# List matmuls moved between turning and multiplying the second listed expert; expert weights reloaded in two steps

## The chip, the cores and the metric

One core of one Trainium2 chip runs the whole program. The metric is the device time of one execution in microseconds (us), the median of three runs. Five engines work side by side, each in its own program order: PE (TensorE), DVE (VectorE), ACT (ScalarE), POOL (GpSimd) and SP (SyncE), which here issues DMAs. They order each other by semaphores that count up (`wait_ge`, `then_inc`). Sixteen DMA engines carry all transfers.

## The reference, cut to what matters

Two layers, 1024 tokens of width 1024, float32. Each layer is a mixer (layer 0: latent attention and a convolution; layer 1: sparse attention) and then a mixture of experts. The change lies in the mixture alone, which both layers run:

```
group   = top 1 of 4 groups by h @ router_group
experts = top 2 of the 8 experts of that group by h @ router_expert
y(token) = sum over its 2 experts e of gate * ((silu(h @ w_gate[e]) * (h @ w_up[e])) @ w_down[e])
x = x + y
```

There are 32 experts with a hidden width of 256. `w_gate[e]`, `w_up[e]` and `w_down[e]` are 1 MB each, so that every layer reads 96 MB of expert weights.

## The kernel before, in words

**Routing.** `route_and_experts` (L1329) first ranks each token inside its expert and sorts the experts by their load. PE's part: 48 matmuls of no use (`spin`, L1323), three matmuls that count tokens (L1657 to L1661), then 16 matmuls of one column for each of the first two experts (L1666) which give the row lists of these two "fast" units early, and 40 more spins. DVE makes one-hot masks (`row_hot`, L1922; `token_hot`; POOL makes `gate_hot`, L1527), and PE multiplies them into the complete lists of rows and gates (32 matmuls at L1679, the "list matmuls"). DVE copies their result to `index` and `gates` (`lists`, L1928 and L1929), and POOL can then gather the rows of all other units.

**Units.** The experts are worked off in 25 units, n = 0 to 24: 18 wide ones (one expert, up to 128 rows) and 7 pairs (two experts, 64 rows each), in the order 4 wide, then seven times (pair, wide, wide). Pairs are units 4, 7, 10, 13, 16, 19 and 22. For a unit PE does:

- `turn_first(n)` (L1572): 8 transposes of the gathered rows, which ACT and DVE copy to `x_cols` (`copy_x`, L1708 and L1715);
- `gate_up(n)` (L1591 wide, L1603 pair): gate and up products. It waits for the whole of the unit's weights (`w_here`, all three transfers) and for the copies;
- `down(n)` (L1633, L1644): the product with `w_down`. ACT and DVE weigh it to `y` (`weigh_y`, L1724 and L1794), and POOL adds `y` to the tokens in DRAM by an indirect DMA (L1489), one such DMA at a time.

In the steady loop the order on PE is gate_up(n+1), turn_first(n+2), down(n). Ahead of it, units 0 and 1 are written out by hand: turn 0, gate_up 0, turn 1, gate_up 1, list matmuls, down 0, turn 2, down 1, gate_up 2, turn 3.

**Weights.** Six buffers of 3 MB hold one expert each. Load i (0 to 31) goes to buffer i % 6; wide units take one load, pairs two. Loads 0 to 5 are issued early. SP then issues load i for i = 6 to 31 as soon as `down_done` tells that the unit that used load i-6 has ended its down product (L1458, L1459): gate, up and down in one go (`load_expert`, L1298). `LOADS[i][0]` is the unit of load i. Load 6 waits for unit 0, load 7 for unit 1, load 8 for unit 2, loads 10 and 11 for unit 4.

**Rows.** Four buffers hold gathered rows. POOL issues the gather of unit n+6 at unit n (`gather_first`, L1474), after the transposes that free the buffer; those of units 2 to 5 directly behind `lists`.

Of the kernel before, what the change touches and what calls it, by code (L numbers as in the profile page):

```python
# [1224 lines left out]
WEIGHT_BUFS = 6  # L1225
# [71 lines left out]

def load_expert(eng, A, layer, e, w, here):  # L1298

    gate, up, down = (A[n][layer] for n in ("moe_w_gate", "moe_w_up", "moe_w_down"))  # L1300
    eng.dma_start(w[:, GATE, :], gate[bass.ds(e, 1)].rearrange("o (p c) f -> p (o c f)", p=P)).then_inc(here, 16)
    eng.dma_start(w[:, UP, :], up[bass.ds(e, 1)].rearrange("o (p c) f -> p (o c f)", p=P)).then_inc(here, 16)
    eng.dma_start(w[:, DOWN, :].rearrange("p (c n) -> p c n", c=2), down[bass.ds(e, 1)].rearrange("o (c p) n -> p (o c) n", p=P)).then_inc(here, 16)


def load_place(eng, A, layer, i, order, w, w_here):

    n, place = LOADS[i]
    e = eng.value_load(order[place:place + 1, 0:1], min_val=0, max_val=EXPERTS - 1)
    load_expert(eng, A, layer, e, w[i % WEIGHT_BUFS], w_here[i % WEIGHT_BUFS])  # L1310

# [10 lines left out]
def spin(pe, ident, spare, count):  # L1322

    for _ in range(count):
        pe.transpose(spare[:, 0:P], ident[:, :], ident[:, :])  # L1325


def route_and_experts(nc, name, layer, logits, w, w_here, ident, ones, index, order, order_ready, more, gates, extra_end, turn_no,
# [8 lines left out]
    with Phase(nc, name) as ph:  # L1337
# [115 lines left out]
        with nc.Block() as block:  # L1453
            @block.sync
            def _(sp):
                loads(sp)
                for i in range(B, EXPERTS):
                    sp.wait_ge(down_done, LOADS[i - B][0] + (LEAD + 1))  # L1458
                    load_place(sp, A, layer, i, order, w, w_here)  # L1459
                if load_next:  # L1460
                    sp.wait_ge(down_done, LAST_SHARED_UNIT + (LEAD + 1))
                    load_next(sp)

                def extra(j):
                    sp.wait_ge(down_done, j + (UNITS + LEAD))
                    e = sp.value_load(more[0:1, bass.ds(j, 1)], min_val=0, max_val=EXPERTS - 1)
                    load_expert(sp, A, layer, e, w[0], w_here[0])

                extras(sp, extra)
# [94 lines left out]
            def _(pe):  # L1564
# [83 lines left out]
                def down(n):  # L1648
                    if paired(n):
                        down_pair(n)  # L1650
                    else:
                        down_wide(n, buffers(n)[0], n % 2)

                spin(pe, ident, spare, 48)
                pe.wait_ge(exps_ready, 3)
# [5 lines left out]
                pe.matmul(rank_ps[:, 0:T * EXPERTS], ones[:, :], so_far[:, :, :].rearrange("p e t -> p (e t)"),  # L1661
                          start=False, stop=True).then_inc(ranked, 1)
                for n in range(FAST):
                    pe.wait_ge(fast_hot_ready, n + 1)
                    for t in range(T):
                        last = pe.matmul(fast_ps[n][:, 0:1], fast_hot[:, n, t, :], token[:, t:t + 1], start=(t == 0), stop=(t == T - 1))  # L1666
                    last.then_inc(fast_listed, 1)
# [3 lines left out]
                turn_first(1)  # L1671
                gate_up(1)
                for k in range(TOP_K):
# [8 lines left out]

                down(0)
                turn_first(2)
                down(1)
                gate_up(2)
                turn_first(3)
                for n in range(FAST, UNITS):
                    if n + 1 < UNITS:
                        gate_up(n + 1)  # L1690
                    if n + 2 < UNITS:
                        turn_first(n + 2)
                    down(n)
                    if n + 1 < UNITS and paired(n + 1):
                        turn_hidden(n + 1)
# [15 lines left out]
            def _(act):  # L1711
# [18 lines left out]
                for n in range(FAST):  # L1730
                    copy_x(act, copy, n, n, 0, x_act)
                    copy_x(act, copy, n, n, 1, x_dve)
                    sigmoid(n, n)
                act.wait_ge(lists, 1)
                weigh_y(0, 0, gates[:, 0:1])
                copy_x(act, copy, 2, 0, 0, x_act)
                weigh_y(1, 1, gates[:, 1:2])
                sigmoid(2, 0)
                copy_x(act, copy, 3, 1, 0, x_act)
                for n in range(FAST, UNITS):  # L1740
                    u = SEQUENCE[n]
                    if n + 1 < UNITS:
                        sigmoid(n + 1, (n + 1) % 2)
                    if n + 2 < UNITS:
                        copy_x(act, copy, n + 2, n % 2, 0, x_act)
                    if n >= 2:
                        act.wait_ge(y_sent, 16 * (n - 1))
# [13 lines left out]
            def _(dve):  # L1761
# [153 lines left out]
                for k in range(TOP_K):  # L1915
# [4 lines left out]
                    for half in range(2):  # L1920
# [3 lines left out]
                                          ).then_inc(row_hot_ready, 1)  # L1924
                for n in range(FAST):
                    hidden(n)
                dve.wait_ge(indexed, 1)
                mine.link(dve.tensor_scalar(index[:, :], index_ps[:, 0:BLOCKS], no_token[:, 0:1], None, ALU.add))  # L1928
                dve.tensor_copy(gates[:, :], index_ps[:, BLOCKS:2 * BLOCKS]).then_inc(lists, 1)  # L1929
                dve.wait_ge(lists, 1)  # L1930
                weigh_y(0, 0, gates[:, 0:1])
                copy_x(dve, dve.tensor_copy, 2, 0, 1, x_dve)
                weigh_y(1, 1, gates[:, 1:2])
                count_extra()
                hidden(2)
                copy_x(dve, dve.tensor_copy, 3, 1, 1, x_dve)
                for n in range(FAST, UNITS):
                    u = SEQUENCE[n]
# [1139 lines left out]
```

## Time and profile before

| | us |
|---|---|
| median of 3 runs | 2223.14 |
| lowest, highest | 2219.01, 2225.81 |
| the profiled execution's own time | 2218.28 |
| its span in the profile | 2216.4 |
| PE busy | 1977.6 (89%) |
| DVE, ACT, POOL busy | 951.6, 701.8, 458.6 |

The profiled execution is one run under the hardware profiler; the time of 1.9 us outside its span is start and end. "Granted clock" is the share of full speed that TensorE was given: 1.00 is 2.4 GHz and 0.50 is 1.2 GHz. "DMA share" is the mean busy share of the 16 DMA engines (it can come out a little above 1). The routing and expert stage of layer 0 stands at about 614 to 979 us, that of layer 1 at about 1853 us to the end. PE's idle time in front of a group stands in square brackets with what ended it; "issue" there means that nothing the profile shows was waited for, and at a pair's first gate_up matmul (L1603) it is the wait for weights to land, which this view does not name.

### The profile page before, as it was taken

What the parts mean: (1) busy time and instruction counts of PE and PEld (TensorE: products, weight loads), DVE (VectorE), ACT (ScalarE), POOL (GpSimd) and SP (SyncE); (2) the same over time, 40 slices, a digit from 0 to 9 for tenths busy, and PEclk for the clock granted to TensorE, in tenths of its full rate; (3) what the DMA queues carried; (4) which work ended last, traced back from release to release, by engine and by line L of the source; (5) the groups of instructions that cost most, each with busy time, mean ns of one, the idle gap of its engine ahead of it and who ended that gap; (6) DMA issues with size and microseconds to landing.
All of it is one profiled execution on the core that took longest, in us unless ns stands there. A gap on an engine that the chain in (4) does not pass through costs nothing. (4 is left out here: it accounts for less than half of the span.)

```text
span 2216.4 us, 30271 instructions
## 1 busy us (share of the span) xinstructions
PE 1977.6 (89%) x11237; PEld 1260.0 (57%) x11237; DVE 951.6 (43%) x2308; ACT 701.8 (32%) x1765; POOL 458.6 (21%) x619
## 2 busy tenths in 40 slices
PE   6999859999989988959999858999999998998987
PEld 3444435655587656545655535666666457675664
DVE  3896874433252211104223486666665126211111
ACT  4013655531111111112122575766776111111111
POOL 0001003321022212110000254554454001221211
PEclk9999969999989999989999888999999998999999
DMA  5000011132568999863000200001000515799993
GB/s 219 0 0 0 0 32 36 39 119 85 233 231 326 377 364 369 314 218 56 1 0 0 80 1 11 11 11 49 11 21 11 205 64 233 270 361 379 362 335 120
DMA packets 80888, 307.77 MB, mean 139 GB/s; under 512 B 18352, under 2 KB 23495, under 8 KB 63846
## 3 DMA queue, kind: packets, MB, share of 16 engines
q1 hardware_dynamic: 66342, 272.23, 31.7%
q0 software_dynamic: 14400, 33.59, 6.1%
q8 instruction: 92, 1.51, 0.3%
q14 instruction: 54, 0.44, 0.1%
HBM read 276.75 MB, written 47.89 MB: 146 GB/s over the span
## 5 line engine op out<-in xcount | busy, mean ns | idle before, releaser
L1112 POOL TENSOR_SCALAR nsaatt_probs<-nsaatt_probs,nsaatt_inv,trunk_gates_or_logits 128x384 f32<-128x384 f32 (+7 forms) x256 | 186.5, 742 | 201.4 <-DVE nsaatt_inv L1139 201.4
L1125 DVE CUSTOM_DVE_ANT_0 nsaatt_probs<-nsaatt_scores,trunk_arena 128x384 f32<-128x384 f32 (+7 forms) x256 | 151.3, 629 | 87.7 <-PE nsaatt_scores L1031 87.4
L1766 DVE TENSOR_TENSOR experts_sig<-experts_gu_ps,experts_sig 128x256 f32<-128x256 f32 x50 | 21.2, 425 | 372.1 <-ACT experts_sig L1720 372.1
L1083 ACT ACTIVATE nsaatt_probs<-nsaatt_probs,nsaatt_bias 128x384 f32<-128x384 f32 (+7 forms) x256 | 169.4, 669 | 11.8 <-DVE nsaatt_bias L1134 11.7
L1591 PE MATMUL experts_gu_ps<-experts_x_cols,ahead 128*128 128x128 f32 x1408 | 161.8, 276 | 5.5 <-ACT experts_x_cols L1715 5.5
L1591 PEld LDWEIGHTS experts_gu_ps<-experts_x_cols,ahead 128*128 128x128 f32 x1408 | 159.1, 192 | 12.1 <-issue 12.0
L1031 PE MATMUL nsaatt_scores<-layer_k_cols,trunk_x_rows 64*128 64x384 f32 (+3 forms) x640 | 131.1, 521 | 15.7 <-DVE nsaatt_top L1125 12.8
L1041 PE MATMUL nsaatt_turn<-trunk_ident,nsaatt_probs 128*128 128x128 f32 x912 | 123.8, 279 | 23.7 <-POOL nsaatt_probs L1112 6.0
L1720 ACT ACTIVATE experts_sig<-experts_gu_ps 128x256 f32<-128x256 f32 x50 | 19.2, 384 | 379.4 <-PE experts_gu_ps L1591 242.1
L1041 PEld LDWEIGHTS nsaatt_turn<-trunk_ident,nsaatt_probs 128*128 128x128 f32 x912 | 97.2, 140 | 57.5 <-issue 36.7
L2250 PE MATMUL nsain_q_ps<-trunk_arena,l1b_h_cols 128*128 128x512 f32 x256 | 111.7, 594 | 0.0
L268 DVE SCALAR_TENSOR_TENSOR l0a_conv<-layer_v_rows,l0a_taps,l0a_conv 128x1024 f32<-128x1024 f32 x87 | 104.8, 1284 | 0.0
L1474 POOL DMA_INDIRECT moe_x<-h_rows,moe_index x46 | 47.7, 1036 | 271.6 <-PE experts_x_ps L1572 240.7
L563 DVE TENSOR_TENSOR trunk_x_rows<-out_acc,trunk_x_rows 128x512 f32<-128x512 f32 x32 | 22.1, 692 | 171.7 <-PE out_acc L491 171.7
L1087 ACT ACTIVATE trunk_arena<-nsaatt_turn 128x512 f32<-128x512 f32 (+1 forms) x136 | 65.8, 515 | 79.6 <-PE nsaatt_turn L1041 78.9
L1031 PEld LDWEIGHTS nsaatt_scores<-layer_k_cols,trunk_x_rows 64*128 64x128 f32 x640 | 55.1, 195 | 60.3 <-issue 37.3
L1724 ACT ACTIVATE trunk_x_rows<-experts_y_ps,moe_gates 128x512 f32<-128x512 f32 x50 | 34.4, 688 | 157.2 <-PE experts_y_ps L1633 99.7
L1054 PE MATMUL nsaatt_values<-trunk_arena,layer_v_rows 128*64 128x128 f32 x1228 | 81.8, 276 | 0.0
L2250 PEld LDWEIGHTS nsain_q_ps<-trunk_arena,l1b_h_cols 128*128 128x128 f32 x256 | 48.2, 190 | 58.0 <-issue 57.9
L1633 PE MATMUL experts_y_ps<-ahead,experts_hid 128*128 128x512 f32 x176 | 79.4, 594 | 2.0 <-DVE trunk_x_rows L1794 2.0
L1031 PE MATMUL mlaatt_scores<-layer_k_cols,trunk_x_rows 96*128 96x512 f32 (+3 forms) x192 | 74.9, 530 | 5.1 <-DVE mlaatt_top L1125 4.1
L1603 PE MATMUL experts_gu_ps<-ahead,experts_x_cols 128*64 128x512 f32 x192 | 61.8, 654 | 19.4 <-issue 19.4
(444 smaller groups left out, 3774.6 us busy)
## 6 DMA issues: line engine op xcount, KB each, us to landing
ahead<-in_moe_w_gate_dram SPq DMA_DIRECT2D x34, 1024.0 KB, 12.0
ahead<-in_moe_w_up_dram SPq DMA_DIRECT2D x34, 1024.0 KB, 16.4
ahead<-in_moe_w_down_dram SPq DMA_DIRECT2D x34, 1024.0 KB, 22.7
trunk_arena<-in_moe_w_gate_dram SPq DMA_DIRECT2D x10, 1024.0 KB, 7.5
trunk_arena<-in_moe_w_up_dram SPq DMA_DIRECT2D x10, 1024.0 KB, 14.1
trunk_arena<-in_moe_w_down_dram SPq DMA_DIRECT2D x10, 1024.0 KB, 23.2
moe_w<-in_moe_w_gate_dram SPq DMA_DIRECT2D x10, 1024.0 KB, 9.6
moe_w<-in_moe_w_up_dram SPq DMA_DIRECT2D x10, 1024.0 KB, 14.5
```

Of the source, the lines that this page charges most:

```text
L268: ins = dve.scalar_tensor_tensor(out=to, in0=shifted, scalar=w, in1=to, op0=ALU.mult, op1=ALU.add)
L1031: last = pe.matmul(scores_of(s, r, h)[:, lo:hi], st["q"][h], br["k"][h](lo, hi), start=True, stop=True)
L1041: last = pe.transpose(t_ps[n % TURNS][:, (h * (hi - lo) + b - lo) * P:(h * (hi - lo) + b - lo + 1) * P], part(s, r, h)[:, b * P:(b + 1) * ...
L1054: last = pe.matmul(o_ps[h * V_DIM:(h + 1) * V_DIM, 0:P], br["v"][h](b), turned_probs[n % PT_BUFS][:, at:at + P], start=(r == 0 and b == 0) ...
L1083: act.activation(part(s, r, h), part(s, r, h), ACT.Exp, bias=bias[:, b, i:i + 1], scale=steps[s]["scale"][h], accum_out=total[:, b, i:i + ...
L1087: return act.activation(to, source, ACT.Copy)
L1112: pool.tensor_scalar(part(s, r, h), part(s, r, h), inv[:, s % BUFS, i:i + 1], 1.0 if gate is None else gate[h], ALU.mult, ALU.mult).then_i ...
L1125: dve.tensor_tensor_reduce(part(s, r, h), scores_of(s, r, h), br["mask"], 1.0, -3e38, ALU.add, ALU.max, top[:, s % BUFS, i:i + 1]).then_in ...
L1591: last = pe.matmul(to, wm[:, c, half * P:(half + 1) * P], x_cols[:, b, c, :], start=(c == 0), stop=(c == CHUNKS - 1))
L1603: last = pe.matmul(gu_ps[b][mine, :].rearrange("p (k f) -> p k f", k=2), x_cols[:, b, c, mine], w[s][:, GATE:UP + 1, c * HIDDEN:(c + 1) * ...
L1633: last = pe.matmul(y_ps[half][:, :], hid[:, b, c * P:(c + 1) * P], wm[:, c, half * BANK:(half + 1) * BANK], start=(c == 0), stop=(c == 1))
L2250: last = pe.matmul(to, h_cols[:, c, t * P:(t + 1) * P], w_in[:, c, lo:hi], start=(c == 0), stop=(c == CHUNKS - 1))
```

## The change

PE's order for units 0 and 1: the list matmuls now stand behind turn 1 and ahead of gate_up 1, and from there the steady loop runs from n = 0 (gate_up 1, turn 2, down 0, gate_up 2, turn 3, down 1, ...). ACT, DVE follow: ACT's sigmoid of unit 1 and DVE's `hidden(1)` move behind `lists`, and DVE makes `count_extra` ahead of it. The first spin goes from 48 to 60 matmuls, and 16 spins are added between the counting matmuls and the one-column matmuls. The reload of a buffer is split: gate and up wait for `gu_done` of the unit that used the buffer, and down, issued behind them on the same queue, for its `down_done`. The whole diff:

```diff
--- before.py
+++ after.py
@@ -1295,19 +1295,21 @@
         eng.wait_ge(self.x_stored, 16 * TILES)
 
 
-def load_expert(eng, A, layer, e, w, here):
+def load_expert(eng, A, layer, e, w, here, down_free=None):
 
     gate, up, down = (A[n][layer] for n in ("moe_w_gate", "moe_w_up", "moe_w_down"))
     eng.dma_start(w[:, GATE, :], gate[bass.ds(e, 1)].rearrange("o (p c) f -> p (o c f)", p=P)).then_inc(here, 16)
     eng.dma_start(w[:, UP, :], up[bass.ds(e, 1)].rearrange("o (p c) f -> p (o c f)", p=P)).then_inc(here, 16)
+    if down_free:
+        eng.wait_ge(*down_free)
     eng.dma_start(w[:, DOWN, :].rearrange("p (c n) -> p c n", c=2), down[bass.ds(e, 1)].rearrange("o (c p) n -> p (o c) n", p=P)).then_inc(here, 16)
 
 
-def load_place(eng, A, layer, i, order, w, w_here):
+def load_place(eng, A, layer, i, order, w, w_here, down_free=None):
 
     n, place = LOADS[i]
     e = eng.value_load(order[place:place + 1, 0:1], min_val=0, max_val=EXPERTS - 1)
-    load_expert(eng, A, layer, e, w[i % WEIGHT_BUFS], w_here[i % WEIGHT_BUFS])
+    load_expert(eng, A, layer, e, w[i % WEIGHT_BUFS], w_here[i % WEIGHT_BUFS], down_free)
 
 
 def load_router(nc, layer, w, bias, here, A):
@@ -1455,8 +1457,9 @@
             def _(sp):
                 loads(sp)
                 for i in range(B, EXPERTS):
-                    sp.wait_ge(down_done, LOADS[i - B][0] + (LEAD + 1))
-                    load_place(sp, A, layer, i, order, w, w_here)
+                    last_use = LOADS[i - B][0] + (LEAD + 1)
+                    sp.wait_ge(gu_done, last_use)
+                    load_place(sp, A, layer, i, order, w, w_here, (down_done, last_use))
                 if load_next:
                     sp.wait_ge(down_done, LAST_SHARED_UNIT + (LEAD + 1))
                     load_next(sp)
@@ -1651,7 +1654,7 @@
                     else:
                         down_wide(n, buffers(n)[0], n % 2)
 
-                spin(pe, ident, spare, 48)
+                spin(pe, ident, spare, 60)
                 pe.wait_ge(exps_ready, 3)
                 pe.wait_ge(carry_made, 2)
                 pe.matmul(rank_ps[:, 0:T * EXPERTS], not_before[:, :], member[:, :, :].rearrange("p e t -> p (e t)"),
@@ -1660,6 +1663,7 @@
                 pe.matmul(total_ps[:, 0:EXPERTS], ones[:, :], so_far[:, :, T - 1], start=True, stop=True).then_inc(ranked, 1)
                 pe.matmul(rank_ps[:, 0:T * EXPERTS], ones[:, :], so_far[:, :, :].rearrange("p e t -> p (e t)"),
                           start=False, stop=True).then_inc(ranked, 1)
+                spin(pe, ident, spare, 16)
                 for n in range(FAST):
                     pe.wait_ge(fast_hot_ready, n + 1)
                     for t in range(T):
@@ -1669,7 +1673,6 @@
                 turn_first(0)
                 gate_up(0)
                 turn_first(1)
-                gate_up(1)
                 for k in range(TOP_K):
                     pe.wait_ge(token_hot_ready, k + 1)
                     pe.wait_ge(gate_hot_ready, k + 1)
@@ -1680,12 +1683,7 @@
                                          start=(k == 0 and t == 0), stop=(k == TOP_K - 1 and t == T - 1))
                 last.then_inc(indexed, 1)
 
-                down(0)
-                turn_first(2)
-                down(1)
-                gate_up(2)
-                turn_first(3)
-                for n in range(FAST, UNITS):
+                for n in range(UNITS):
                     if n + 1 < UNITS:
                         gate_up(n + 1)
                     if n + 2 < UNITS:
@@ -1730,19 +1728,16 @@
                 for n in range(FAST):
                     copy_x(act, copy, n, n, 0, x_act)
                     copy_x(act, copy, n, n, 1, x_dve)
-                    sigmoid(n, n)
-                act.wait_ge(lists, 1)
-                weigh_y(0, 0, gates[:, 0:1])
-                copy_x(act, copy, 2, 0, 0, x_act)
-                weigh_y(1, 1, gates[:, 1:2])
-                sigmoid(2, 0)
-                copy_x(act, copy, 3, 1, 0, x_act)
-                for n in range(FAST, UNITS):
+                    if n == 0:
+                        sigmoid(0, 0)
+                for n in range(UNITS):
                     u = SEQUENCE[n]
                     if n + 1 < UNITS:
                         sigmoid(n + 1, (n + 1) % 2)
                     if n + 2 < UNITS:
                         copy_x(act, copy, n + 2, n % 2, 0, x_act)
+                    if n == 0:
+                        act.wait_ge(lists, 1)
                     if n >= 2:
                         act.wait_ge(y_sent, 16 * (n - 1))
                     weigh_y(n, n % 2, gates[:, u:u + 1])
@@ -1922,19 +1917,13 @@
                         dve.tensor_tensor(row_hot[:, k, part], over(row_no[:, :].unsqueeze(1), (P, HALF_TILES, P)),
                                           over(row_f[:, k, part].unsqueeze(2), (P, HALF_TILES, P)), ALU.is_equal
                                           ).then_inc(row_hot_ready, 1)
-                for n in range(FAST):
-                    hidden(n)
+                hidden(0)
                 dve.wait_ge(indexed, 1)
                 mine.link(dve.tensor_scalar(index[:, :], index_ps[:, 0:BLOCKS], no_token[:, 0:1], None, ALU.add))
                 dve.tensor_copy(gates[:, :], index_ps[:, BLOCKS:2 * BLOCKS]).then_inc(lists, 1)
                 dve.wait_ge(lists, 1)
-                weigh_y(0, 0, gates[:, 0:1])
-                copy_x(dve, dve.tensor_copy, 2, 0, 1, x_dve)
-                weigh_y(1, 1, gates[:, 1:2])
                 count_extra()
-                hidden(2)
-                copy_x(dve, dve.tensor_copy, 3, 1, 1, x_dve)
-                for n in range(FAST, UNITS):
+                for n in range(UNITS):
                     u = SEQUENCE[n]
                     if n + 1 < UNITS:
                         hidden(n + 1)
```

## Rows read from the trace of the kernel before

**Rows 1.** The page: busy time of each engine:

```profile
PE 1977.6 (89%) x11237; PEld 1260.0 (57%) x11237; DVE 951.6 (43%) x2308; ACT 701.8 (32%) x1765; POOL 458.6 (21%) x619
```

**Rows 2.** Waits, PE in both expert stages (us in total, times, longest):

```profile
PE experts_gu_ps L1603 <- issue: 20.2, 5, 9.2
...
PE experts_gu_ps L1603 <- issue: 18.8, 5, 7.0
```

**Rows 3.** Timeline of PE, layer 0: start, length, line, [idle before]:

```profile
614.24 6.95 PE L1325 MATMUL experts_gu_ps<-trunk_ident 128*128 128x128 f32 x48 [1.10 <-PEq L448]
621.02 0.64 PE L1657 MATMUL experts_y_ps<-experts_member,experts_not_before 128*128 128x256 f32 x2
...
624.19 3.57 PE L1666 MATMUL experts_hid_ps<-experts_token,trunk_x_rows 128*128 128x1 f32 x16 [1.58 <-DVE trunk_x_rows L1858]
627.63 3.55 PE L1666 MATMUL experts_index_ps<-experts_token,trunk_x_rows 128*128 128x1 f32 x16
631.04 6.20 PE L1325 MATMUL experts_gu_ps<-trunk_ident 128*128 128x128 f32 x40
637.08 1.04 PE L1572 MATMUL experts_x_ps<-trunk_ident,moe_x 128*128 128x128 f32 x8
...
649.15 7.38 PE L1591 MATMUL experts_gu_ps<-experts_x_cols,ahead 128*128 128x128 f32 x64 [1.38 <-ACT experts_x_cols L1715]
656.37 3.70 PE L1679 MATMUL experts_index_ps<-trunk_arena,trunk_x_rows 128*128 128x86 f32 x32
659.90 3.63 PE L1633 MATMUL experts_y_ps<-ahead,experts_hid 128*128 128x512 f32 x8
665.70 1.16 PE L1572 MATMUL experts_x_ps<-trunk_ident,moe_x 128*128 128x128 f32 x8 [2.17 <-DMA moe_x<-h_rows,moe_index]
...
679.64 7.38 PE L1591 MATMUL experts_gu_ps<-experts_x_cols,trunk_arena 128*128 128x128 f32 x64 [1.31 <-DVE experts_x_cols L1708]
```

**Rows 4.** Timeline of PE, the same stretch of layer 1:

```profile
1864.76 1.95 PE L1666 MATMUL experts_hid_ps<-experts_token,trunk_x_rows 128*128 128x1 f32 x16 [1.52 <-DVE trunk_x_rows L1858]
...
1876.05 1.04 PE L1572 MATMUL experts_x_ps<-trunk_ident,moe_x 128*128 128x128 f32 x8
...
1904.84 1.16 PE L1572 MATMUL experts_x_ps<-trunk_ident,moe_x 128*128 128x128 f32 x8 [2.34 <-DMA moe_x<-h_rows,moe_index]
```

**Rows 5.** Windows, long stretches and clock, layer 0; last row layer 1:

```profile
628.00:630.00 2.00, 2.00 (x11) 0.50 0.00 0
648.00:720.00 72.00, 67.38 (x458) 1.00 0.76 276
720.00:808.00 88.00, 77.73 (x475) 0.96 1.02 377
...
1864.00:1866.00 2.00, 1.24 (x11) 1.00 1.05 438
```

**Rows 6.** Timeline of DVE and SP in layer 0: last row mask, first reloads:

```profile
645.54 1.85 DVE L1922 TENSOR_TENSOR trunk_x_rows<-experts_row_no,experts_row_f 128x512 f32<-128x512 f32 x2
...
664.28 0.34 SPq L1301 DMA_DIRECT2D ahead<-in_moe_w_gate_dram  x1
...
692.09 0.34 SPq L1301 DMA_DIRECT2D ahead<-in_moe_w_gate_dram  x1
```

**Rows 7.** Windows: length, PE busy, granted clock, DMA share, GB/s; layer 0:

```profile
640.00:648.00 8.00, 7.77 (x70) 1.00 1.02 414
656.00:664.00 8.00, 7.54 (x45) 1.00 0.09 17
680.00:696.00 16.00, 16.00 (x101) 1.00 0.77 280
```

**Rows 8.** DMA issues of 640 to 960 us: count, median us to landing:

```profile
moe_x<-h_rows,moe_index POOLq DMA_INDIRECT x23, 8.5
```

**Rows 9.** Timeline of PE, layer 0: pairs of units 10 and 13:

```profile
762.44 7.09 PE L1603 MATMUL experts_gu_ps<-ahead,experts_x_cols 128*64 128x512 f32 x32 [1.05 <-issue]
...
806.86 1.09 PE L1603 MATMUL experts_gu_ps<-moe_w,experts_x_cols 128*64 128x512 f32 x1 [9.22 <-issue]
```

## The prediction, made before the changed kernel ran

> **What bounds the kernel now.** I read the page first: PE is busy 89% of the span [rows 1], so what counts is where PE still waits. The list of waits over the two expert stages gives one large group: pairs whose first gate_up matmul stands for 20.2 us in layer 0 and 18.8 us in layer 1, five times each [rows 2]. These are waits for weights. The timeline of PE then shows three short holes at the head of the units [rows 3]: 1.38 us ahead of gate_up 1 (copies of the turned rows; gate_up 0, which is not touched, waits alike), 2.17 us ahead of turn 2 (the gather that could only start behind the lists), 1.31 us ahead of gate_up 3 (copies again). Layer 1 has the same holes, with 2.34 us at turn 2 [rows 4]. Last the DMA windows: from 720 to 808 us the DMA engines are full (share 1.02) while PE is not, and before that, 648 to 720, they stand at 0.76 [rows 5]. So the stage has two regimes: a head set by PE's order, and behind it a stretch set by how early the weight transfers were started.
>
> **Part 1, list matmuls ahead of gate_up 1.** Turn 1 ends at 649.15 - 1.38 = 647.77 [rows 3]. The last row mask is ready at 645.54 + 1.85 = 647.39 [rows 6], so the list matmuls can start at once. They take 659.90 - 656.37 = 3.53 us, and the 1.38 us of copies of unit 1 lie under them: that hole goes. Copies of unit 3 lie under down 1 in the new order, as in the loop: the 1.31 us goes. Turn 2 now comes behind gate_up 1 (656.37 - 649.15 = 7.22 us). Before, it started 665.70 - 659.90 = 5.80 us after the end of the lists, with the DMA engines idle (share 0.09 from 656 to 664 [rows 7]); 5.80 is under 7.22, so with this landing time 2.17 us goes too. Removed: 4.86 us in layer 0, 1.38 + 2.34 + 1.31 = 5.03 us in layer 1.
>
> The cover is thin, 1.4 us. The gathers over the whole stage take a median of 8.5 us [rows 8], and the first reload now runs beside these four. The gather of unit 2 took 4.3 us at the idle engines; with 8.5 it would come 4.2 us later, and PE would stand 4.2 - 1.4 = 2.8 us. I take 1.5 us of new wait per layer (only gate and up of one load are in flight), between 0 and 2.8. `hidden(1)` and `count_extra` ahead of it on DVE lie under gate_up 1 and cost nothing; the weighing of unit 0 follows them and is needed only by down 1, one gate_up later.
>
> The Trainium skill bears on this place, page "DMA: Bandwidth & Descriptors", section "Issuing engines are not separate DMA queues": transfers started by SP and by GpSimd run on the same 16 engines and interleave. It speaks against the change, and the trace agrees: 4.3 us idle, 8.5 us in the median. By that rule the 2.8 us would be due in both layers, and at its worst it is the slower rival below.
>
> **Part 2, spins.** The counting matmuls start when the 48 spins end: 621.02 - 614.24 = 6.78 us, 0.141 each. Twelve more cost 1.7 us, on the path, since DVE's masks wait for the counts. The 16 spins (2.3 us) fill the 1.58 us hole ahead of the one-column matmuls [rows 3] and overrun it by some 0.5 us. The one-column matmuls then start up to 1.7 + 0.5 = 2.2 us later; so I take it for layer 1, and 1.8 for layer 0, where some 0.4 us of counting was a wait for DVE. Against that stands the clock: in layer 0 it was 0.50, 1.2 GHz [rows 5], and the 32 took 631.04 - 624.19 = 6.85 us; in layer 1 it was 1.00 at first [rows 5] and the first 16 took 1.95 us [rows 4], so 32 of them take 3.9 us at 2.4 GHz. The 40 spins behind them took 6.04 us, 5.7 at full clock. All warm: layer 0 gains 2.95 + 0.35 - 1.8 = 1.5 us; layer 1, where the one-column matmuls and spins took 1876.05 - 1864.76 = 11.3 us and would take 3.9 + 5.7 = 9.6, loses 2.2 - 1.7 = 0.5. All cold as before: they lose 1.8 and 2.2. I take layer 0 -1.1 and layer 1 +0.8 (the clock still falls somewhere in the run), together -0.3; both ends kept: -1.0 to +4.0. The gather of unit 0 is no obstacle: like unit 2's it needs some 4.3 us and PE spins past it.
>
> **Part 3, reload in two steps.** Gate and up of load 6 leave when gate_up 0 is done, about 647, not at 664.28 [rows 6]. Its down waits for down 0, at nearly the old time. From then on SP is one unit ahead: gate and up of load 7 leave right behind down 6, those of load 8 when down 1 ends, about 674, against 692.09 [rows 6]. The new wait in front of each down holds back the next load's gate and up, but these would have waited for the same unit or a later one before. No transfer leaves later except by PE's order (down 1 now ends some 3 us later: load 7's last third).
>
> What is it worth? Loads arrive at the pace of full engines from 720 on, so an arrival moves forward by the DMA work that is now done in what was idle: in 648 to 720 that idle is (1.02 - 0.76) x 72 / 1.02 = 18.4 us [rows 5]. Filled are: 2.1 MB of gate and up at 414 GB/s [rows 7] = 5.1 us; some 1 us from load 7; the idle of 680 to 696, (1.02 - 0.77) x 16 / 1.02 = 3.9 us [rows 7], by load 8. Sum 10.0 us. The pair of unit 13, which waited 9.22 us after 1.05 us at unit 10 [rows 9], had 10.3 us of waits, and PE reaches it 3 to 5 us sooner by part 1, so the DMA decides there and unit 13 starts 10 us sooner. Behind it the remaining waits, 20.2 - 10.3 = 9.9 us in layer 0, stand in a stretch where the engines are full most of the time. There PE, being earlier, meets the same transfers, and a part of the lead turns back into waiting. I take 7.5 us left at the end of the stage. The ends: 3 us (part 1 alone survives, all else is waited for again) and 14 us (a few of the later waits shrink also). Part 1 and 2 do not add to this: they are what PE would bring if weights were no bound (4.86 - 1.5 + 1.1 = 4.5 in layer 0, 5.03 - 1.5 - 0.8 = 2.7 in layer 1), and only the later of PE and weights counts. Layer 1 shows the same waits, so the same 7.5 us.
>
> **Sum.** 2 x 7.5 = 15 us off the profiled execution's 2218.3: 2203. That execution was 4.9 us below the median of the runs (2223.1), so against the median 2208.1, my forecast. A difference under 0.3% (6.7 us) can't be told from none.
>
> **Rivals.**
>
> - *The weights give it back.* All waits behind the head grow by what PE arrives sooner, since the bytes are the same and the buffers too: 2 x 3 = 6 us gained, 2217. For it: share 1.02 over 88 us. Against it: 18 us of idle engines ahead of it.
> - *Nothing comes through.* The DMA work of the whole stage is the bound, and the early idle is refilled by slower gathers and adds (8.5 against 4.3 us): 2223. For it the full engines, against it that the adds are not awaited by PE in the rows.
> - *Weight waits nearly vanish.* If the later buffers too are filled in idle gaps, up to 14 or 15 us per layer: 2194. Against it: 6 buffers as before, and loads still wait for all three parts.
> - *Slower.* The early reload sits in front of the four gathers. At 12 us to landing instead of 4.3 unit 2's rows come 7.7 - 1.4 = 6.3 us late, which eats the 4.9 us, and with cold one-column matmuls (+4.0 in both layers) and the late head handed on through every down_done: 2 x (6.3 - 4.9) + 4.0 = 7 us, 2230. It decides if the gather takes over 10.6 us (4.3 + 1.4 + 4.9) and the weights give nothing. For it: the thin cover, and 8.5 us as the median. Against it: only gate and up of one load are in flight, and one queue's gather stands first.
>
> The Trainium skill, page "TensorE: Matmul & The Clock Gate", section "What's actually happening", says that the throttled state is the default and activity releases it. By it the added spins hold the one-column matmuls warm, the -1.0 end of part 2. The trace agrees in that 0.50 stands behind a hole of PE; whether one-column matmuls count as activity no row shows.
>
> **How the numbers follow.** Forecast (gain of 8 to 25 us): 0.66. Given back (about 6 us, half of it beyond 0.3%): 0.12. Nothing: 0.07. Waits vanish: 0.08. Slower: 0.07. Faster is 0.66 + 0.08 + 0.06 = 0.80, same 0.06 + 0.07 = 0.13, slower 0.07. The range, 2196 to 2217, runs from a gain of 27 us, just short of the rival at 2194, to the giving back; it leaves out slower, nothing and part of the farthest gain, some 0.2 in all.
>
> **What would show it.** Right: gate_up 1 without a hole directly behind 3.5 us of list matmuls; turn 2 behind gate_up 1 with under 2.8 us; gate of load 6 at about 647 on SP; DMA share of 648 to 720 near 0.9; unit 13 some 10 us sooner, with a wait of about 4 us less or more; granted clock of 1.00 through the one-column matmuls. Wrong: gathers of over 10 us at unit 2; the sum of pair waits at or above 20 us per layer; turn 0 later by 2 us in both layers; a stage end that moved by 3 us or less though unit 13 moved by 10.

## The result, and the profile after

The changed kernel took 2204.26 us, median of 5 runs (2202.24 to 2209.84), against 2222.68 us for the kernel before, a difference of the medians of 18.4 us. The ratio, taken over all the runs and not from the two medians, is 0.9926, 95% interval 0.9912 to 0.9940: faster by some 16 us (13 to 20), where 15 were forecast. The profiled execution took 2202.24 us with a span of 2200.4, 16.0 us less than before.

The list of waits of PE in the changed kernel, first layer 0, then layer 1 (us in total, times, longest), answers to [rows 2]:

```profile
PE experts_gu_ps L1606 <- issue: 14.9, 4, 6.9
...
PE experts_gu_ps L1606 <- issue: 14.4, 4, 6.1
```

The waits for weights are 5.3 and 4.4 us shorter, and one fewer in each layer. The timeline of PE in layer 0 (start, length, line, and in brackets the idle time before) answers to [rows 3]:

```profile
614.31 8.29 PE L1327 MATMUL experts_gu_ps<-trunk_ident 128*128 128x128 f32 x60 [1.10 <-PEq L448]
...
623.53 1.91 PE L1327 MATMUL experts_gu_ps<-trunk_ident 128*128 128x128 f32 x16
625.28 1.89 PE L1670 MATMUL experts_hid_ps<-experts_token,trunk_x_rows 128*128 128x1 f32 x16
627.02 2.91 PE L1670 MATMUL experts_index_ps<-experts_token,trunk_x_rows 128*128 128x1 f32 x16
629.79 6.89 PE L1327 MATMUL experts_gu_ps<-trunk_ident 128*128 128x128 f32 x40
636.52 1.04 PE L1575 MATMUL experts_x_ps<-trunk_ident,moe_x 128*128 128x128 f32 x8
...
647.03 3.70 PE L1682 MATMUL experts_index_ps<-trunk_arena,trunk_x_rows 128*128 128x86 f32 x32
650.57 7.34 PE L1594 MATMUL experts_gu_ps<-experts_x_cols,ahead 128*128 128x128 f32 x64
660.04 1.16 PE L1575 MATMUL experts_x_ps<-trunk_ident,moe_x 128*128 128x128 f32 x8 [2.12 <-DMA moe_x<-h_rows,moe_index]
...
675.94 7.31 PE L1594 MATMUL experts_gu_ps<-experts_x_cols,trunk_arena 128*128 128x128 f32 x64
```

gate_up 1 (650.57) and gate_up 3 (675.94) carry no bracket any more: both copies lie under other work. Turn 2 still waits for its gather, 2.12 us here and 1.10 in layer 1. SP's issues and POOL's first gather in layer 0 show why:

```profile
647.07 0.34 SPq L1301 DMA_DIRECT2D ahead<-in_moe_w_gate_dram  x1
647.50 0.38 SPq L1302 DMA_DIRECT2D ahead<-in_moe_w_up_dram  x1
664.67 0.38 SPq L1305 DMA_DIRECT2D ahead<-in_moe_w_down_dram  x1
...
677.30 0.34 SPq L1301 DMA_DIRECT2D ahead<-in_moe_w_gate_dram  x1
```

```profile
652.04 1.03 POOL L1477 DMA_INDIRECT moe_x<-h_rows,moe_index  x1 [6.45 <-DVE moe_gates L1923]
```

Gate and up of load 6 leave at 647.07 ([rows 6]: 664.28), those of load 8 at 677.30 (692.09). The gather of unit 2 was issued at 652.04 and let turn 2 go at 660.04, 8.0 us later (7.0 in layer 1); before it took 4.3 us at idle engines. Windows of layer 0 (length, PE busy, granted clock, DMA share, GB/s) answer to [rows 5]:

```profile
626.00:628.00 2.00, 2.00 (x19) 0.94 0.36 145
628.00:630.00 2.00, 2.00 (x11) 0.50 0.00 0
...
648.00:720.00 72.00, 69.88 (x478) 1.00 0.89 317
720.00:808.00 88.00, 84.34 (x486) 0.96 1.02 379
```

The DMA share of 648 to 720 us rose from 0.76 to 0.89. Unit 13, which waited 9.22 us until 806.86 [rows 9], now starts at 796.29, 10.6 us sooner (11.0 in layer 1, counted from the first spin):

```profile
796.29 1.09 PE L1606 MATMUL experts_gu_ps<-moe_w,experts_x_cols 128*64 128x512 f32 x1 [3.66 <-issue]
```

### The profile page after: what moved, and what is told of

Same layout as the page of the kernel before. It is cut to its first block and busy times, and to the rows that moved or that the text cites. A ratio compares the mean times of both kernels' runs of the same rounds, so it can differ in the third digit from the quotient of the medians.

```text
span 2200.4 us, 30381 instructions
## 1 busy us (share of the span) xinstructions
PE 1979.2 (90%) x11293; PEld 1263.0 (57%) x11293; DVE 951.5 (43%) x2308; ACT 701.0 (32%) x1765; POOL 457.3 (21%) x619
## 5 line engine op out<-in xcount | busy, mean ns | idle before, releaser
L1031 PE MATMUL nsaatt_scores<-layer_k_cols,trunk_x_rows 64*128 64x384 f32 (+3 forms) x640 | 131.1, 521 | 15.7 <-DVE nsaatt_top L1125 12.8
L1718 ACT ACTIVATE experts_sig<-experts_gu_ps 128x256 f32<-128x256 f32 x50 | 19.2, 383 | 369.3 <-PE experts_gu_ps L1594 242.5
L1031 PEld LDWEIGHTS nsaatt_scores<-layer_k_cols,trunk_x_rows 64*128 64x128 f32 x640 | 55.1, 195 | 60.4 <-issue 37.1
L1789 DVE TENSOR_SCALAR trunk_x_rows<-experts_y_ps,moe_gates 128x512 f32<-128x512 f32 x50 | 37.4, 748 | 94.6 <-PE experts_y_ps L1636 32.6
## 6 DMA issues: line engine op xcount, KB each, us to landing
ahead<-in_moe_w_gate_dram SPq DMA_DIRECT2D x34, 1024.0 KB, 14.3
moe_w<-in_moe_w_gate_dram SPq DMA_DIRECT2D x10, 1024.0 KB, 12.5
```

The source lines that it names most:

```text
L1031: last = pe.matmul(scores_of(s, r, h)[:, lo:hi], st["q"][h], br["k"][h](lo, hi), start=True, stop=True)
```

## The experiments

Whole runs scatter by some 5 us, also for reasons outside the experts: the stretch from the last down product of layer 0 to the first spin of layer 1, which no experiment touches, took 886.5 to 892.4 us in the profiles. So beside the ratio I read the length of the stage: first of the opening spins to the end of the last down product, from the first and last PE rows of each profiled run. "Pair waits" is the row of the waits shown above, "turn 2" the wait in brackets there. There is one profile for each kernel, and it can stray: with the old spins the stages came out 3.9 and 2.9 us longer than in the changed kernel, with 16 spins 0.9 and 3.1, and neither ratio is worse. The changed kernel's profile is also the fastest of its five runs, that of "first load whole" the slowest of its six. So stage differences of 3 or 4 us are not to be leaned on unless the ratio goes with them.

| kernel | ratio to before, 95% interval | stage, layer 0 / 1 | pair waits | turn 2 |
|---|---|---|---|---|
| before | 1 | 352.2 / 349.2 | 20.2 / 18.8 | 2.2 / 2.3 |
| changed | 0.9926 (0.9912 to 0.9940) | 342.4 / 339.7 | 14.9 / 14.4 | 2.1 / 1.1 |
| order alone | 0.9952 (0.9938 to 0.9966) | 344.6 / 342.8 | 19.1 / 17.5 | 0 / 0 |
| reload alone | 0.9954 (0.9938 to 0.9970) | 346.5 / 346.3 | 14.7 / 13.8 | 2.2 / 2.0 |
| old spins | 0.9921 (0.9907 to 0.9935) | 346.3 / 342.6 | 15.8 / 16.0 | 2.6 / 0.7 |
| first load whole | 0.9928 (0.9915 to 0.9941) | 343.5 / 342.5 | 17.9 / 19.1 | 0 / 0 |
| first load alone early | 0.9980 (0.9968 to 0.9992) | 349.9 / 348.8 | 20.7 / 18.7 | 2.5 / 2.8 |
| half of w_down | 0.9742 (0.9722 to 0.9762) | 324.6 / 323.4 | none | 2.8 / 2.6 |
| down apart | 0.9915 (0.9895 to 0.9934) | 341.8 / 338.1 | 12.8 / 12.7 | 2.6 / 0.8 |
| 16 spins | 0.9916 (0.9898 to 0.9933) | 343.3 / 342.8 | 15.6 / 14.3 | 2.8 / 2.7 |
| gate alone early | 0.9916 (0.9900 to 0.9932) | 342.6 / 341.0 | 18.1 / 15.7 | 0 / 1.4 |
| pairs late | 0.9915 (0.9900 to 0.9931) | 343.9 / 338.1 | 14.2 / 12.5 | 2.6 / 1.3 |
| pairs late, down apart | 0.9888 (0.9871 to 0.9906) | 341.1 / 336.6 | 12.4 / 10.8 | 2.5 / 2.6 |

**Order alone.** The changed kernel with the reload of before:

```diff
-                    sp.wait_ge(gu_done, last_use)
-                    load_place(sp, A, layer, i, order, w, w_here, (down_done, last_use))
+                    sp.wait_ge(down_done, last_use)
+                    load_place(sp, A, layer, i, order, w, w_here)
```

> The changed order of PE, ACT and DVE and the changed spins, but each load again leaves whole, behind down_done. Theory A (both parts count, because at the pair of unit 13 the later of PE and weights decides and each part moves the weights a little): the head is 4 to 5 us per layer earlier, down_done comes earlier and with it the loads, so 8 to 10 us less than before: a ratio of 0.9955 to 0.9965. Rival B (the head alone makes the gain, the split reload is worth nothing): the whole 0.9926. Rival C (the weights alone make it): 1.000, the head's 5 us per layer are waited for again at units 13 to 22. In the trace: PE's wait for weights at pairs stays near 20 us per layer under A, grows to 25 under C.

Measured 0.9952: some 11 us of the 16, a little more than theory A's 8 to 10. The pair waits stay near 20, as theory A has it, and the stage is 7.6 and 6.4 us shorter. B and C both lie outside the interval. Unit 13 starts 185.4 us after the first spin of the stage (615.97), where it was 192.6 before and is 182.0 in the changed kernel:

```profile
801.33 1.09 PE L1606 MATMUL experts_gu_ps<-moe_w,experts_x_cols 128*64 128x512 f32 x1 [8.78 <-issue]
```

Its windows of layer 0 beside [rows 5] (columns as there):

```profile
648.00:720.00 72.00, 72.00 (x494) 1.00 0.85 298
720.00:808.00 88.00, 78.47 (x460) 0.94 1.02 381
```

The idle share ahead of 720 us went from 0.26 to 0.17 with the loads still leaving whole: 0.09 x 72 / 1.02 = 6.4 us of transfers done earlier. The same sum for the others, from their own rows of 648 to 720 us, beside the shortening of the layer 0 stage: changed 0.89, 9.2 us (stage 9.8); first load whole 0.88, 8.5 (8.7); order alone 0.85, 6.4 (7.6); reload alone 0.82, 4.2 (5.7); first load alone early 0.81, 3.5 (2.3); old spins 0.86, 7.1 (5.9); 16 spins 0.88, 8.5 (8.9); gate alone early 0.91, 10.6 (9.6); pairs late 0.86, 7.1 (8.3). It does not come out where `gate_up` no longer waits for the whole load (and can't where fewer bytes are moved, as in half of w_down): down apart 0.86, 7.1 (10.4), pairs late with down apart 0.85, 6.4 (11.1). In layer 1, over the same stretch counted from the first spin, the whole-load kernels agree within 3.3 us only.

**Reload alone.** The kernel before, with `load_expert` and SP's loop of the changed kernel and nothing else:

```diff
-                    sp.wait_ge(down_done, LOADS[i - B][0] + (LEAD + 1))
-                    load_place(sp, A, layer, i, order, w, w_here)
+                    last_use = LOADS[i - B][0] + (LEAD + 1)
+                    sp.wait_ge(gu_done, last_use)
+                    load_place(sp, A, layer, i, order, w, w_here, (down_done, last_use))
```

> The kernel before with its own order and spins, and only the reload in two steps. Theory A: gate and up of load 6 leave at 647 instead of 664, loads arrive 5 to 8 us earlier, the holes at the head stay: 10 to 12 us less, a ratio of 0.9945 to 0.9955; PE's waits for weights fall from 20 to 12 to 15 us per layer. Rival B: 1.000. Rival C: the whole 0.9926.

Measured 0.9954, with pair waits of 14.7 and 13.8 us; B and C lie outside the interval. Each part alone gives some 10 us; together they give 16. The sum of the two, 0.0094, and the 0.0074 of both lie 0.0020 apart with some 0.0026 of uncertainty, so an overlap is likely in layer 0 (stages 7.6 and 5.7, together 9.8) but not shown by the whole runs, and layer 1 shows none (6.4 and 2.9, together 9.5). Neither part covers the other. Unit 13 starts 186.2 us after the first spin (615.84) here, 6.4 us sooner than before:

```profile
802.05 0.61 PE L1606 MATMUL experts_gu_ps<-moe_w,experts_x_cols 128*64 128x512 f32 x1 [3.90 <-issue]
```

**First load whole.**

```diff
+                    if i == B:
+                        sp.wait_ge(down_done, last_use)
+                        load_place(sp, A, layer, i, order, w, w_here)
+                        continue
                     sp.wait_ge(gu_done, last_use)
```

> The changed kernel, but load 6 leaves whole behind down 0, so the DMA engines stay idle from about 651 to 661 as before; loads 7 to 31 still leave in two steps. Theory A: the wait at turn 2 goes (2.1 us in layer 0, 1.1 in layer 1), but 5.1 us of early transfers per layer are lost to all later loads: 5 to 8 us slower than the changed kernel, 0.995 to 0.996. Rival E (the lead of one unit that SP holds from load 7 on is what counts, and the first load's early start is given back): within 2 us of the changed kernel, 0.992 to 0.9935.

Measured 0.9928: theory A, which had 5 to 8 us lost, is refuted, and rival E holds. The wait at turn 2 is gone, as it is under "order alone", so the 2 MB in front of the gathers make it. The loads behind lose nothing by the late start: without that wait the gate of load 8 leaves 60.4 us after the first spin, in the changed kernel 63.0.

**First load alone early.**

```diff
+                    if i > B:
+                        sp.wait_ge(down_done, last_use)
+                        load_place(sp, A, layer, i, order, w, w_here)
+                        continue
                     sp.wait_ge(gu_done, last_use)
```

> The changed kernel, but only load 6 leaves in two steps, loads 7 to 31 leave whole behind down_done. With the kernel of whole first load and the one of order alone it makes four corners. The stages of the profiled runs took, layers 0 and 1: 342.4 and 339.7 us (all in two steps), 343.5 and 342.5 (first whole), 344.6 and 342.8 (none in two steps). Theory I (the first load's 5 us are given back because the loads behind it wait for buffers anyway): 344 and 342, the same as none in two steps, ratio 0.9945 to 0.9955. Theory A as predicted (the 5.1 us stay): 340 and 338 or less by the first load alone, ratio 0.992 to 0.993.

Neither: 0.9980, slower than order alone by some 6 us, just more than both intervals allow, with stages 5.3 and 5.9 us longer. With order alone and its DMA windows of layer 0 beside it, the reason can be read. Order alone:

```profile
648.00:664.00 16.00, 16.00 (x123) 1.00 0.62 211
664.00:680.00 16.00, 16.00 (x123) 1.00 0.89 318
```

First load alone early, its windows and SP's issues:

```profile
648.00:664.00 16.00, 13.55 (x112) 1.00 0.81 314
664.00:680.00 16.00, 16.00 (x108) 1.00 0.52 148
```

```profile
666.34 0.38 SPq L1305 DMA_DIRECT2D ahead<-in_moe_w_down_dram  x1
678.53 0.34 SPq L1301 DMA_DIRECT2D ahead<-in_moe_w_gate_dram  x1
```

The two stages start within 0.4 us of each other. The first 16 us move more (0.81 against 0.62), and the next 16 lose 0.37 of theirs: after down 6 at 666.34 nothing could be issued until down 1 was done, at 678.53, where order alone issued load 7 at 675.94. The idle time was moved, not filled, and the wait of 2.45 us at turn 2 came on top and held back each `down_done`: counted from the first spin, load 7 and load 8 (gate at 689.99) leave 3.0 us later than under order alone. Which part of the loss is the wait's and which the emptier engines', these two profiles do not separate.

**Gate alone early.** Of load 6 only gate leaves early; its up waits with its down (`down_free` with a third entry, `i == B`):

```diff
+    if down_free and down_free[2]:
+        eng.wait_ge(*down_free[:2])
     eng.dma_start(w[:, UP, :], up[bass.ds(e, 1)]...
...
```

> The changed kernel, but of load 6 only gate (1 MB) leaves at gate_up 0's end; its up and down wait for down 0. Theory K (the 2 MB in front of the four gathers make PE wait at turn 2: 2.1 and 1.1 us in the changed kernel, 0 with the whole load 6 held back, 2.5 and 2.8 with load 6 alone early): the wait at turn 2 falls to 0 to 1 us, and half of the early start stays: the time is that of the changed kernel within 2 us, the stages 341 to 343 and 339 to 342 us. Rival L (the gathers are slow for their own number, not for the loads in front): the wait at turn 2 stays at 1 to 2.5 us.

0.9916, which can't be told from the changed kernel, with stages of 342.6 and 341.0 us, as K has them. In layer 0 the wait at turn 2 went from 2.1 us to none (the gather was issued at 651.3 and turn 2 started without a wait at 657.1, 5.8 us later at most). In layer 1 it took 7.2 us and 1.4 us of wait are left, no less than the 1.1 of the changed kernel, so K is borne out in one layer only. Layer 1 also varies by itself: with the same 2 MB in front the table has 0.7 to 2.8 us there.

**Half of w_down.**

```diff
     if down_free:
         eng.wait_ge(*down_free)
+        eng.dma_start(w[:, DOWN, 0:D], down[bass.ds(e, 1)]...[:, 0, :]).then_inc(here, 16)
+        return
```

> The changed kernel, but of w_down of loads 6 to 31 only the first half (0.5 MB instead of 1 MB) is transferred, so the second half of the down products uses stale weights; PE's work is unchanged. 26 x 0.5 MB less per layer is some 34 us of full DMA engines against the 15 us that PE waits for weights. Theory A (the stretch behind the head is set by DMA work): PE's waits at pairs fall from 15 to under 3 us per layer, the cold clock behind them goes too: 26 to 34 us less than the changed kernel, a ratio of 0.977 to 0.981. Rival F (latency and buffers set it: a load can't leave before its buffer is free, and what follows takes its time whatever its size): waits of 8 us or more stay, 0.985 or above.

0.9742, below even theory A's range. No pair waits any more; all that is left of PE's waits in layer 0 (list of waits, 612 to 940 us) is:

```profile
PE experts_x_ps L1577 <- DMA moe_x<-h_rows,moe_index: 2.8, 1, 2.8
PE experts_gu_ps L1596 <- ACT experts_x_cols L1715: 1.4, 1, 1.4
PE experts_gu_ps L1329 <- PEq L448: 1.1, 1, 1.1
PE experts_y_ps L1638 <- DVE trunk_x_rows L1791: 1.0, 1, 1.0
```

The stages fall by 17.8 and 16.3 us, a little more than the pair waits. So in the changed kernel the amount of weights sets the stretch behind the head; F is refuted. The ratio says some 41 us less than the changed kernel and the stages 34; the rest is not explained. This also shows what PE's own order takes when no pair waits: some 324 us per stage, with the waits of the head still in it.

**16 spins** ahead of turn 0 (`SPIN = 16`).

> The changed kernel with 16 instead of 40 spins ahead of turn 0. The gather of unit 0 landed 4.5 us behind its issue at 628.5, at 633.0, and the spins held turn 0 back to 636.5: turn 0 can start 3 us sooner. Theory A (at unit 13 the later of PE and weights decides, and it is the weights): the head's gain reaches the end with 1 us per layer or less: within 2 us of the changed kernel. Rival B (PE's order at the head makes the gain): 3 us per layer, 6 us less, 0.990. Rival H (the clock falls while PE waits for the gather): gate_up 0 at 0.50 takes up to 14 us, 5 us or more slower than the changed kernel.

Turn 0 came 3.3 and 2.3 us sooner after the start of the stage, and the stages are not shorter. The ratio is 0.9916 (0.9898 to 0.9933): A's bound and, barely, B's 0.990 both lie inside the interval, so B is not refuted by it. Nor was B's condition kept up: turn 2 waits longer (2.8 and 2.7 us) and starts 2.0 us sooner in layer 0 and 1.0 us later in layer 1 than in the changed kernel. H came in one layer. In layer 0 the clock, already at 0.50 since the one-column matmuls, rose again at turn 0 and stood at 1.00 before gate_up 0. In layer 1 it fell again behind turn 0, and gate_up 0 took 9.01 us in place of 7.38 (windows: length, PE busy, granted clock, DMA share, GB/s):

```profile
632.00:634.00 2.00, 2.00 (x12) 0.50 0.38 115
634.00:636.00 2.00, 1.59 (x9) 0.71 0.59 141
636.00:638.00 2.00, 1.03 (x9) 1.00 0.79 319
...
1866.00:1868.00 2.00, 0.97 (x6) 0.85 0.76 233
1868.00:1870.00 2.00, 2.00 (x11) 0.50 1.02 401
```

**Old spins** (60 back to 48, the 16 in the middle taken out).

> The changed kernel with the spins of before: 48 and none in the middle, 40 at the end. Theory A: turn 0 moves by 0 to 2 us in either direction and the weights decide the end of the stage anyway: 0.992 to 0.9935, the same as the changed kernel; the one-column matmuls run at 0.50 again and take 6.9 us. Rival D (the warm clock is a part of the gain): turn 0 comes 1 to 2 us later in both layers and it reaches the end: 0.9935 to 0.9945.

0.9921 against 0.9926: the spins are worth nothing that can be measured, theory A. Turn 0 came 0.7 and 1.5 us later after the first spin. The one-column matmuls took 632.62 - 625.98 = 6.6 us again instead of 4.5.

**Down apart.** `gate_up` waits for gate and up alone; for loads 6 to 31 down lands on a semaphore of its own:

```diff
-                    pe.wait_ge(w_here[s], use * 48)
+                    pe.wait_ge(w_here[s], use)          # 48 + 32 * (i // B)
...
                 def down(n):
+                    wait_down(n)                         # held.d_here[i % B]
```

> The changed kernel, but gate_up waits only for gate and up of loads 6 to 31, and down for its own transfer (a semaphore of its own). Loads land some 11 us apart, a third of it is down. Theory A (a pair waits for the arrival of the last transfer it asks for): each pair starts some 3.5 us sooner against the arrivals, once per layer and not once per pair: 2 x 3.5 = 7 us less than the changed kernel, 0.989 to 0.990. Rival G (the bytes alone set the end): within 2 us of the changed kernel, 0.992 to 0.9935, because down then waits for what gate_up no longer waits for.

0.9915, between rival G's range and theory A's, and the interval reaches into both: 0.6 and 1.6 us shorter stages, well short of the 3.5 per layer of theory A. Its interval overlaps the changed kernel's, so no gain is shown.

**Pairs late.**

```diff
-        take = 2
+        take = (3, 3, 2, 2, 2, 2, 0)[n]
```

> The changed kernel with the pairs at units 4, 8, 12, 15, 18, 21 and 24 instead of 4, 7, 10, ... 22: the same experts, later where two loads are asked for at once. Theory A (a unit starts when its last load has landed, and the loads land at the pace of the DMA work): in the changed kernel's layer 0 load 29 landed at 917.7 and unit 22, with 39 us of PE work from there, ended the stage at 956.7. With the pairs late, the last pair needs load 31 (landed at 935.3) and has some 16 us behind it: 951, and no earlier pair asks for more; 5 to 6 us less per layer, 0.987 to 0.989. Rival J (buffers come free later when pairs come later, the loads land later by as much): within 2 us of the changed kernel, 0.992 to 0.9935.

0.9915, just under J's range, which the interval overlaps, and clear of A's: layer 0 was 1.5 us longer, layer 1 1.6 us shorter. The assumption that the loads keep their times failed: the last pair of layer 0 started at 942.25 behind a wait of 2.65 us, where the expectation had its load landed at 935.3 (the stage began 1.6 us later).

**Pairs late, down apart.**

> Pairs late as in the other kernel, and gate_up waits for gate and up alone, down for its own transfer. Theory A: the last load binds the last unit, and its gate and up land some 3 us ahead of its down, so 1 to 3 us per layer less than pairs late alone: 0.985 to 0.988. Rival G (bytes alone): the same as pairs late alone.

0.9888, 2197.36 us (2192.71 to 2201.59): apart from the kernel that leaves out half of w_down the only faster version whose interval lies clear of the changed kernel's, some 8 us faster than it. The two edits one by one gave 2 to 3 us each; with intervals of 3 to 4 us to either side that the two together give more than their sum is not shown. G's "the same as pairs late alone" is not excluded either, since those two intervals overlap.

## Why the prediction was right

The forecast was 2208 (a gain of 15 us) and the measured gain is 16; by its own steps:

- *Part 1* held in place and size. List matmuls at 647.03 (forecast 647.8), the 1.38 and 1.31 us gone, a new wait at turn 2 of 2.1 and 1.1 us where 1.5 was taken between 0 and 2.8 (0.7 to 2.8 over the kernels with the same loads in front). The cause given, the first reload in front of the gathers, is shown: without that reload the wait is 0 in both layers, with gate alone 0 in one.
- *Part 2* came out near the forecast with a detail off. From the first spin to turn 0 layer 0 took 636.52 - 614.31 = 22.2 us instead of 22.8, layer 1 0.3 us less than before; -1.1 and +0.8 were taken. The first 16 one-column matmuls ran at 1.00 in both layers, but then the clock fell to 0.50, and the 40 spins took 6.9 us in place of 6.2. The price of a spin was read wrong: 0.141 us is the mean over 48 spins of which the first ran at 0.50 (rows of 614 to 618 us); the 16 added ones, at 1.00, took 625.28 - 623.53 = 1.75 us and not 2.3. In the run with the old spins no effect of the term on the whole time can be seen.
- *Part 3*: unit 13 started 10.6 us sooner, 10.0 forecast, with 3.7 us of wait left, about 4 forecast. Less was given back behind it than was taken: the stages are 9.8 and 9.5 us shorter, not 7.5. From these 19.2 us the whole span kept 16.0; the stretch between the stages, untouched, took 2.9 us more in this execution (890.3 against 887.4), which is inside its scatter.
- *The failed statement: "Part 1 and 2 do not add to this".* By the prediction the reload decides and the order of PE is covered by it, so that order alone would leave about 3 us a layer. It gives 7.6 and 6.4 us of stage, as much as the reload by itself (5.7 and 2.9) or more. The reason is in the windows under "order alone" and in SP's issues there: with `down_done` of units 2, 3 and on coming sooner, the gates of loads 8 and 9 leave 6.4 us sooner after the first spin than before (687.40 and 698.97 against 692.09 and 703.63, with a stage that begins 1.7 us later), and fill idle time without any reload in two steps.
- *One term stood for the wrong thing.* "2.1 MB of gate and up at 414 GB/s = 5.1 us" was booked as filled idle time of load 6 for itself. With the new order given, the four corners are: nothing in two steps 344.6 / 342.8 us, load 6 alone 349.9 / 348.8, loads 7 to 31 alone 343.5 / 342.5, all 342.4 / 339.7. So sending gate and up of load 6 early costs 5.3 and 5.9 us of stage where load 7 can't follow (some 6 us in the whole runs). Where it can, the profiles say 1.1 and 2.8 us, and the whole runs nothing (0.9926 against 0.9928), not 5.1 per layer. The 10.0 us of the sum were booked to the reload alone; by itself the reload moved unit 13 by 6.4 us, the order by itself by 7.2, both by 10.6. So the total came near because the reload was priced too high and the order's share was left out of the same sum: two errors of opposite sign, and in that the closeness of 15 to 16 is luck.
- *The rivals.* "The weights give it back" would have left 3 us per layer, the stages lost 9.8 and 9.5. "Nothing" and "vanish" are refuted by the same row. "Slower" had to begin at 10.6 us for the gather of unit 2; it took 8.0 in layer 0, behind 2 MB issued 4.5 to 5 us ahead of it. The Trainium skill, page "DMA: Bandwidth & Descriptors", section "Issuing engines are not separate DMA queues", says that transfers started by different engines run on the same 16 DMA engines and interleave; the trace agrees in direction (4.3 us without a load in front, 8.0 with one).

What stays open: whether "pairs late" and "down apart" give more together (0.9888) than the two alone, and why; whether the order and the reload overlap; and how far the waits behind unit 13 are set by single loads, since only sums were read there.

## What to carry to other kernels

Ask of a transfer that starts early whether the next one in the same queue can follow it. Here the first load alone early lost some 6 us, because the idle time of the DMA engines moved from before it to behind it and PE waited for the gathers behind the burst; and even where load 7 could follow, the early start of load 6 by itself gained nothing that the whole runs show. So count the idle DMA time that a change fills up to the point from which the engines are full, not the early bytes of one load. In layer 0 that number and the shortening of the stage agreed within 1.5 us for the nine kernels that move all the weights and in which PE waits for whole loads, and failed by 3 and 5 us for the two in which it does not. And where PE's order and the transfers each release the other, price the two edits separately and together: here about 10 us each and 16 in all.

## What the hardware showed that was not expected

- Gathers of unit 2's rows, from POOL's issue to PE's start on them, layer 0: 4.3 us with the engines idle, at most 5.8 with gate of one load in front of it, 8.0 with gate and up. In layer 1 the last two are 7.2 and 7.0, so the step from one to two transfers in front is seen in one layer only. The median over the stage stayed at 8.5 us in the changed kernel.
- A wait can cost more than itself. With the old spins turn 2 of layer 0 waited 2.57 us, the granted clock of 664 to 666 us was 0.50, and down 0 took 5.22 us; in the changed kernel the wait was 2.12 us and down 0 took 3.60. With 16 spins, layer 1, it was 2.65 and 5.29. Nothing in the prediction priced this.

```profile
662.89 1.26 PE L1575 MATMUL experts_x_ps<-trunk_ident,moe_x 128*128 128x128 f32 x8 [2.57 <-DMA moe_x<-h_rows,moe_index]
663.95 5.22 PE L1636 MATMUL experts_y_ps<-ahead,experts_hid 128*128 128x512 f32 x8
```

- The clock can fall while PE has no gap. In the changed kernel it was 0.94 in the window of 626 to 628 us and 0.50 in the next, both with 2.00 of 2.00 us busy: the fall lies inside the run of one-column matmuls, behind the first 16 of them (1.89 us; 3.57 before, at 0.50). In layer 1 the same, 0.99 and then 0.50 at 1860 us. In both layers the clock was at 1.00 again before gate_up 0. The Trainium skill, page "TensorE: Matmul & The Clock Gate", section "What's actually happening", says that activity releases the throttle. Here the clock rose during the first spins (0.50 at 614 us, 1.00 at 618) and fell during the one-column matmuls, with PE busy in both. That a PE busy with one-column matmuls does not hold the clock is the reading nearest to these rows; no run tested it by itself.
- Full DMA engines are no proof that PE waits. Half of w_down, window of 720 to 808 us, has PE busy for all of it at a DMA share of 1.00. With down apart, where all the weights are moved, PE is busy for all 88.00 us too, at a share of 1.02. Half of w_down:

```profile
720.00:808.00 88.00, 88.00 (x521) 1.00 1.00 361
```
